# Routed experts of a decoder step: four lanes of 64 rows, or three lanes of 64 and two of 32

## What is computed

```python
def swiglu(x, w_gu, w_down):
    g, u = jnp.split(x @ w_gu, 2, axis=-1)
    return (jax.nn.silu(g) * u) @ w_down
...
yb = lax.map(lambda a: swiglu(a[0], w_e_gu[a[1]], w_e_down[a[1]]), (xb, block_expert))
y = jnp.zeros((N + 1, D), x.dtype).at[slot_token].add(yb.reshape(n_slots, D) * slot_gate[:, None])
```

## Time and profile before

| what | us |
|---|---|
| median of 3 runs | 2894.19 |
| lowest, highest | 2887.44, 2895.16 |
| the profiled execution | 2892.4 |
| its span, first to last instruction | 2890.6 |
| dispatch stage, about | 1858.4 to 1995.4 |
| routed stage, about | 1995.4 to 2791 |
| combine stage | from 2791 on |

### The profile page before, as it was taken

How to read it: one execution, slowest core, us unless ns; L and a number is a source line. 1 busy time by engine, 2 the same in 40 slices (tenths; PEclk the granted TensorE clock), 3 DMA queues, 4 the chain that set the end, 5 groups by cost and what they waited for, 6 DMA issues and landing times. The chain is left out here.

```text
span 2890.6 us, 44067 instructions
## 1 busy us (share of the span) xinstructions
PE 2560.4 (89%) x14550; PEld 1473.9 (51%) x14550; DVE 1507.3 (52%) x3758; ACT 1106.3 (38%) x2384; POOL 372.8 (13%) x419
## 2 busy tenths in 40 slices
PE   4998996979989799986889959797999999999977
PEld 1443443558878687874566634344333333333332
DVE  1456554658878778784888664585111111111126
ACT  1223212659878688783655501121111111111110
POOL 0000000111011000101232121043000000000025
PEclk7999997979999999996999979898999999999988
DMA  8023058622154021207100084215989899897867
GB/s 332 17 77 93 21 159 288 215 82 74 56 200 165 35 76 41 88 1 181 43 26 18 9 270 131 104 44 230 407 330 420 335 352 343 315 386 274 312 248 283
DMA packets 192864, 511.69 MB, mean 177 GB/s; under 512 B 24169, under 2 KB 102315, under 8 KB 160440
## 3 DMA queue, kind: packets, MB, share of 16 engines
q1 hardware_dynamic: 136812, 311.88, 30.2%
q0 software_dynamic: 28640, 127.09, 12.2%
q10 hardware_dynamic: 27252, 70.69, 6.5%
HBM read 631.86 MB, written 86.93 MB: 249 GB/s over the span
## 5 line engine op out<-in xcount | busy, mean ns | idle before, releaser
L2974 PE MATMUL routed_ex_pG<-dispatch_exWG,routed_ex_XT 128*64 128x512 f32 x2048 | 451.1, 597 | 12.8 <-DMA dispatch_exWG<-in_w_e_gu 10.7
L2097 DVE TENSOR_REDUCE ssqc<-SQ 128x8 f32<-128x512 f32 x516 | 346.1, 683 | 116.7 <-ACT SQ L1900 102.5
L1805 PE MATMUL eK<-dWkv,LT 128*128 128x256 f32 x1032 | 316.4, 389 | 12.3 <-ACT SQ L1900 11.8
L1808 PE MATMUL eK<-WA,LT 128*128 128x272 f32 x1032 | 326.9, 399 | 0.0
L1900 ACT ACTIVATE SQ<-eK 128x512 f32<-128x512 f32 x516 | 292.2, 602 | 56.1 <-PE eK L1808 41.2
L2974 PEld LDWEIGHTS routed_ex_pG<-dispatch_exWG,routed_ex_XT 128*64 128x64 f32 x2048 | 147.5, 138 | 310.7 <-issue 310.3
L3065 DVE TENSOR_TENSOR routed_ex_sg<-routed_ex_sg,routed_ex_pG 128x256 f32<-128x256 f32 x64 | 26.9, 421 | 525.9 <-ACT routed_ex_sg L3022 525.9
L556 PE MATMUL in_pp<-ada_Win,in_hT 128*128 128x512 f32 (+1 forms) x640 | 280.7, 597 | 9.8 <-ACT in_pr L454 9.8
L2993 PE MATMUL routed_ex_pY<-routed_ex_WD,routed_ex_AT 128*64 128x512 f32 x1024 | 233.8, 598 | 0.8 <-DMA routed_ex_WD<-in_w_e_down 0.8
L1808 PEld LDWEIGHTS eK<-WA,LT 128*128 128x128 f32 x1032 | 200.7, 194 | 28.9 <-DVE numc L2096 0.2
L1805 PEld LDWEIGHTS eK<-dWkv,LT 128*128 128x128 f32 x1032 | 189.6, 195 | 47.7 <-ACT SQ L1900 17.0
(11 more groups left out here) (551 smaller groups left out, 3738.6 us busy)
## 6 DMA issues: line engine op xcount, KB each, us to landing
dispatch_exWG<-in_w_e_gu SPq DMA_DIRECT2D x256, 1024.0 KB
routed_ex_WD<-in_w_e_down SPq DMA_DIRECT2D x132, 1024.0 KB, 13.0
s_yblk<-routed_ex_Y ACTq DMA_DIRECT2D x64, 512.0 KB
ada_Win<-in_w_ada ACTq DMA_DIRECT2D x8, 2048.0 KB, 12.7
s_yblk<-zrows SPq DMA_DIRECT2D x15, 1024.0 KB
ada_Wada<-in_w_ada SPq DMA_DIRECT2D x8, 1024.0 KB, 15.3
ada_Win<-in_w_in ACTq DMA_DIRECT2D x4, 2048.0 KB, 18.7
dispatch_exWG<-in_w_e_gu SPq DMA_DIRECT2D x4, 2048.0 KB
```

Of the source, the lines that this page charges most:

```text
L1805: pe.matmul(pK[kn % 3][:, 512 + z:512 + z + HK], key, Wkv[:, 4:8, 0:NOPE], start=True, stop=True)
L1808: pe.matmul(pK[kn % 3][:, z:z + HK + 16], key, WA[:, pr, :], start=True, stop=True).then_inc(s_KN, 1)
L2097: dve.tensor_reduce(ssqc[cg % 2][:, n - 1 - tau, :], SQ[kn % 4].rearrange("p (h d) -> p h d", h=H), AX.X, ALU.add).then_inc(s_red, 1)
L2974: m = pe.matmul(pG[u][r, :], XT[u][:, k, r], WG[2 * u + v][:, k, :], start=(k == 0), stop=(k == KD - 1))
```

## The change

Each pair has five lanes: three of 64 rows and two of 32. Block 0 holds lanes 0 and 1 (64 rows each), block 1 holds lane 2 (64 rows) and lanes 3 and 4 (32 rows each, at rows 64 and 96). An expert is cut either into tiles of 64 rows, and goes to the wide lanes, or into tiles of 32, and goes to the narrow ones. Experts with an even number of 32-row tiles stand first in an order, those with an odd number last; the chip computes for every possible dividing point how many pairs the wide and the narrow lanes would need, takes the point where the larger of both is least, and that is `nq`. Positions in the two lists are kept apart by adding `CLASS` to those of the narrow list, and the block and row of each token are computed for both lists and one of them chosen. The largest number of pairs, `NQ`, becomes 46, `NBLK` 92. The first gate/up weights of the fifth lane are loaded at the beginning of the routed stage, ahead of the down weights. Two tensors (`SD`, `lg`) are no longer kept for the whole program, and two of the nine matrices B have a place of their own, which frees and takes SBUF.

The diff, cut to its core:

```diff
@@ -40,8 +40,14 @@
 NEG = -3.0e38
 NC9 = NS + 1
 GRP = 64
-NQ = -(-(NE + (NTOK * TK - NE) // GRP) // 4)
+TILE = 32
+N64, N32 = 3, 2
+NL = N64 + N32
+NQ = -(-(NE + (NTOK * TK - NE) // GRP + -(-NTOK // GRP)) // 4) + 1
 NQ += NQ % 2
+LANE_ROWS = [(v // 2, GRP * (v % 2), GRP) for v in range(N64)] + [(1, GRP * (N64 - 2) + TILE * w, TILE) for w in range(N32)]
+LANES = [[v for v in range(NL) if LANE_ROWS[v][0] == u] for u in range(2)]
+CLASS = 16384
 NBLK = 2 * NQ
 SLOTS = NBLK * P
 BIGM = 1.0e9
...
-        G["expert"] = sb("expert", [5, P], I32)
-        G["loads"] = sb("loads", [1, 4 * NQ], I32)
+        G["expert"] = sb("expert", [NL + 1, P], I32)
+        G["loads"] = sb("loads", [1, NL * NQ], I32)
-        G["SD"] = sb("SD", [P, NS // 2, PAGE + 1])
...
+            if st is stage_prompt:
+                scores_kept = root.enter_context(ExitStack())
+                G["SD"] = scores_kept.enter_context(nc.sbuf_tensor("SD", [P, NS // 2, PAGE + 1], F32, side="right"))
+            if st is stage_out:
+                logits_kept = root.enter_context(ExitStack())
+                G["lg"] = logits_kept.enter_context(nc.sbuf_tensor("lg", [P, NT + 1, NE], F32, side="right"))
...
-            for v in range(4):
+            for v in range(NL):
                 sp.dma_start(G["loads"][0:1, v * NQ:(v + 1) * NQ], G["expert"][v:v + 1, 0:NQ]).then_inc(s_m, 16)
-            sp.dma_start(G["nblk"][0:1, 0:1], G["expert"][4:5, 0:1]).then_inc(s_m, 16)
-            sp.wait_ge(s_m, 80)
+            sp.dma_start(G["nblk"][0:1, 0:1], G["expert"][NL:NL + 1, 0:1]).then_inc(s_m, 16)
+            sp.wait_ge(s_m, 16 * (NL + 1))
             expert = [sp.value_load(G["loads"][0:1, v * NQ:v * NQ + 1], min_val=0, max_val=NE - 1) for v in range(4)]
             sp.wait_ge(s_lt, 1)
             for v in range(4):
...
-            link(dve.tensor_scalar(nbi[:, :], nb[:, :], float(GRP - 1), None, ALU.add))
-            link(dve.tensor_scalar(nbi[:, :], nbi[:, :], 6, None, ALU.arith_shift_right))
-            link(dve.tensor_copy(nb[:, :], nbi[:, :]))
-            link(dve.tensor_tensor_scan(be[:, :], ones[:, :], nb[:, :], 0.0, ALU.mult, ALU.add))
-
-            link(dve.tensor_scalar(nqi[:, :], be[:, NE - 1:NE], 3.0, None, ALU.add))
-            link(dve.tensor_scalar(nqi[:, :], nqi[:, :], 2, None, ALU.arith_shift_right))
-            link(dve.tensor_copy(nq[:, :], nqi[:, :]))
-            for v in range(4):
-                link(dve.tensor_scalar(reach[:, v:v + 1], nq[:, :], float(v), c("part"), ALU.mult, ALU.add))
-                link(dve.tensor_scalar(S1[:, 0, :], be[:, :], reach[:, v:v + 1], 0.0, ALU.is_le, ALU.add, accum_out=eb[:, v:v + 1]))
-                link(dve.tensor_scalar(S1[:, 0, :], be[:, :], reach[:, v:v + 1], 0.0, ALU.is_equal, ALU.add, accum_out=first[:, v:v + 1]))
-            link(dve.tensor_scalar(eb[:, 0:4], eb[:, 0:4], float(NE - 1), None, ALU.min))
+            pair = lambda v: v.unsqueeze(1).to_broadcast([P, 2, NE])
+            for x, (g, bits) in enumerate(((GRP, 6), (TILE, 5))):
+                link(dve.tensor_scalar(nbi[:, :], nb[:, :], float(g - 1), None, ALU.add))
+                link(dve.tensor_scalar(nbi[:, :], nbi[:, :], bits, None, ALU.arith_shift_right))
+                link(dve.tensor_copy(size[:, x, :], nbi[:, :]))
+            link(dve.tensor_scalar(nbi[:, :], nbi[:, :], 1, None, ALU.bitwise_and))
+            link(dve.tensor_copy(odd[:, :], nbi[:, :]))
+            link(dve.tensor_tensor(cum[:, :, :], size[:, :, :], pair(odd[:, :]), ALU.mult))
+            for x in range(2):
+                link(dve.tensor_tensor_scan(odds[:, x, :], ones[:, :], cum[:, x, :], 0.0, ALU.mult, ALU.add))
+            link(dve.tensor_tensor(cum[:, :, :], size[:, :, :], cum[:, :, :], ALU.subtract))
+            for x in range(2):
+                link(dve.tensor_tensor_scan(evens[:, x, :], ones[:, :], cum[:, x, :], 0.0, ALU.mult, ALU.add))
+            last = slice(NE - 1, NE)
+            link(dve.tensor_tensor(total[:, :], evens[:, 1, last], odds[:, 1, last], ALU.add))
+            link(dve.tensor_tensor(cum[:, :, :], odds[:, :, :], evens[:, :, :], ALU.subtract))
+            link(dve.tensor_tensor(cum[:, :, :], cum[:, :, :], evens[:, :, last].to_broadcast([P, 2, NE]), ALU.add))
+            link(dve.tensor_tensor(cum[:, :, :], cum[:, :, :], pair(odd[:, :]), ALU.mult))
+            link(dve.tensor_tensor(cum[:, :, :], cum[:, :, :], evens[:, :, :], ALU.add))
+
+            link(dve.tensor_scalar(nbi[:, :], cum[:, 0, :], float(N64 - 1), {2: 256.0, 3: 171.0}[N64], ALU.add, ALU.mult))
+            link(dve.tensor_scalar(nbi[:, :], nbi[:, :], 9, None, ALU.arith_shift_right))
+            link(dve.tensor_copy(cost[:, :], nbi[:, :]))
+            link(dve.tensor_scalar(rest[:, :], cum[:, 1, :], total[:, 0:1], -1.0, ALU.subtract, ALU.mult))
+            link(dve.tensor_scalar(nbi[:, :], rest[:, :], float(N32 - 1), None, ALU.add))
+            link(dve.tensor_scalar(nbi[:, :], nbi[:, :], N32 // 2, None, ALU.arith_shift_right))
+            link(dve.tensor_copy(rest[:, :], nbi[:, :]))
+            link(dve.tensor_tensor(cost[:, :], cost[:, :], rest[:, :], ALU.max))
+            link(dve.tensor_scalar(cost[:, :], cost[:, :], -1.0, None, ALU.mult))
+            link(dve.tensor_reduce(nq[:, :], cost[:, :], AX.X, ALU.max, negate=True))
+
+            link(dve.tensor_scalar(left[:, :], nq[:, :], float(N64), None, ALU.mult))
+            link(dve.tensor_scalar(wide[:, :], cum[:, 0, :], left[:, 0:1], None, ALU.is_le))
+            link(dve.tensor_tensor(rest[:, :], size[:, 1, :], wide[:, :], ALU.mult))
+            link(dve.tensor_reduce(kept[:, :], rest[:, :], AX.X, ALU.add))
+            link(dve.tensor_scalar(cum[:, 1, :], cum[:, 1, :], kept[:, 0:1], None, ALU.subtract))
...
+            link(dve.tensor_tensor(here, each(start[:, :]), at, ALU.is_equal))
+            link(dve.tensor_tensor(here, here, inside, ALU.mult))
+            link(dve.tensor_reduce(first[:, :], here, AX.X, ALU.add))
+            link(dve.tensor_tensor(here, each(start[:, :]), at, ALU.is_le))
+            link(dve.tensor_tensor(here, here, inside, ALU.mult))
+            link(dve.tensor_tensor(here, here, each(c("iota")[:, 0:NE]), ALU.mult))
+            link(dve.tensor_reduce(eb[:, 0:NL], here, AX.X, ALU.add))
...
+            for x, (g, n) in enumerate(((GRP, N64), (TILE, N32))):
+                for v in range(1, n):
+                    link(dve.tensor_scalar(cut[:, N64 * x + v:N64 * x + v + 1], nq[:, :], float(g * v), None, ALU.mult))
+                link(dve.tensor_scalar(back[:, x:x + 1], nq[:, :], -2.0 * P, float(g), ALU.mult, ALU.add))
...
+            for x, (g, n, to) in enumerate(((GRP, N64, place), (TILE, N32, posf))):
+                k = 2 * P // g
+                link(dve.tensor_scalar(part[:, :, :], slot[:, :, :], g - 1, None, ALU.bitwise_and))
+                link(dve.tensor_copy(lane[:, :, :], part[:, :, :]))
+                link(dve.tensor_scalar(to[:, :, :], low[:, :, :], float(k), float(x * GRP * N64), ALU.mult, ALU.add))
+                link(dve.scalar_tensor_tensor(out=to[:, :, :], in0=lane[:, :, :], scalar=float(1 - k), in1=to[:, :, :], op0=ALU.mult, op1=ALU.add))
+                for v in range(1, n):
+                    link(dve.tensor_scalar(lane[:, :, :], low[:, :, :], cut[:, N64 * x + v:N64 * x + v + 1], back[:, x:x + 1], ALU.is_ge, ALU.mult))
+                    link(dve.tensor_tensor(to[:, :, :], to[:, :, :], lane[:, :, :], ALU.add))
...
+    WG = G["ex_WG"] + [sb(f"{pre}WG{i}", [P, KD, 2 * DE]) for i in range(4, NL)]
+    WD = [sb(f"{pre}WD{i}", [P, 2, D]) for i in range(NL)]
...
+    rows_of = [slice(a, a + w) for _, a, w in LANE_ROWS]
...
-                load = [sp.value_load(G["loads"][0:1, bass.ds(i * 2 + (v * NQ + j), 1)], min_val=0, max_val=2 * NE - 1) for v in range(4)]
+                load = [sp.value_load(G["loads"][0:1, bass.ds(i * 2 + (v * NQ + j), 1)], min_val=0, max_val=2 * NE - 1) for v in range(NL)]
                 for u in range(2):
                     for m, (used, landed) in enumerate(((s_gh, s_w), (s_gu, s_wb))):
                         sp.wait_ge(used, i * 4 + (2 * j + u + 3))
-                        for v in (2 * u, 2 * u + 1):
+                        for v in LANES[u]:
                             if m == 0:
-                                sp.wait_ge(G["s_wg"][v], 16)
+                                sp.wait_ge(s_wg0[v], 16)
...
+                for v in range(NL):
+                    sp.wait_ge(s_y, i * 8 + (4 * j + 2 * LANE_ROWS[v][0] + 5))
...
+            expert = [sp.value_load(G["loads"][0:1, v * NQ:v * NQ + 1], min_val=0, max_val=NE - 1) for v in range(NL)]
+            for v in range(4, NL):
+                sp.dma_start(WG[v][:, :, :], T["w_e_gu"][0, bass.ds(expert[v], 1)].rearrange("a (p k) n -> p (a k) n", p=P)).then_inc(s_wg0[v], 16)
+            for v in range(NL):
...
-                    for v in range(2):
```

(51 more changed lines are left out.)

53 lines of the change are left out of this document (28 added, 25 removed).

## The result

The changed kernel takes 3238.1 us (median of 4 runs, 3237.2 to 3250.4), the kernel before 2890.8 us in the runs made beside it. The ratio is 1.120, its 95% interval 1.118 to 1.122: 12% slower. The profiled execution took 3237.9 us, its span is 3236.0.

What follows compares the result with a forecast made beforehand. PE was taken to bound the routed loop, DMA close behind. 2892.4 - 774.3 (old loop) + 1116 (thirty pairs) + 10 (start) + 3 (end) gave 3247, 3249 against the median; forecast 3248 us, range 2830 to 3300.

Steps and rivals of the forecast that it cites:

- both main cases: Routed loop: either a shape change empties PE (chance 0.70, about 3248 us) or lanes run side by side (0.25, 2844 us).
- Pairs: Routed loop: the new plan needs 30 pairs instead of 32, removing 47.1 us if a pair still takes 23.56.
- A pair: Routed loop: a pair takes 37.2 us instead of 23.56, thirty take 1116.
- step: One k of block 1's matmuls: a wide and a narrow phase, together 1.99 us against 0.86, 12 times a pair.
- The decisive choice: Block 1's matmuls: PE empties itself whenever the shape changes, as at single changes in the earlier trace; chance 0.70.
- Weights: Expert weight loads in the routed loop: SP works 14.2 us a pair, no waits for weights, 0 us added.
- Dispatch: DVE's planning before the routed loop: chain 17 us instead of 6.2, B ending some 20 us later.
- The start of the loop: First routed weights and gate_up after dispatch: +10 us, bounds 0 (all covered) and +20 (none).
- The loop's end: Skipped rounds between the last store's issue and combine, 8 instead of 4: +3 us, bounds 0 and +6.
- (a): Block 1: narrow lanes run beside the wide one, pair stays 23.56 us; 2844 us, range 2830 to 2870; chance 0.25.
- (b): Block 1: the narrow lanes too come one after another, 49 us a pair, total 3605 us; chance 0.03.
- (c): Routed loop: the saving does not come, through another dividing point or late first weights; about 2893 us; chance 0.02.

Runs made afterwards that it cites:

- all32: Changed kernel with the 64 rows of lane 2 issued as two matmuls of 32, so block 1 has one shape: 2861.9 us, ratio 0.988.
- before_block1_split: The control: kernel before, with both lanes of block 1 issued as two matmuls of 32 rows each, one shape: 2907.8 us.
- lanes24: Changed kernel with two lanes of 64 in block 0, four of 32 in block 1, part of z moved through DRAM: 2832.7 us, ratio 0.979.
- down_mixed: Changed kernel with lane 2 issued in 32s in gate_up alone; down still mixes 64 and 32: 2974.8 us.
- grouped: Changed kernel, block 1 reordered: in each half of gate_up and down all wide-lane steps first, then all narrow ones: 3171.6 us.
- before_lane3_split: Kernel before, with only the second lane of block 1 issued as two matmuls of 32 beside one of 64: 3304.5 us.
- all32_nopool: Changed kernel with block 1 all in 32s, without POOL's products for the shared expert's output; leaves work out: 2841.0 us.

## Why the prediction was right

Forecast 3248, measured 3238; faster was given 0.26 and slower 0.73. The stated range, 2830 to 3300, held both main cases, so its being met says little; what tells is the pair, its step and the rows of the profile.

**Pairs.** 30 forecast, 30 measured. **A pair.** 37.2 forecast, 36.94 measured; step 1.99 forecast, 1.99 in the rows above. The decisive choice, that the gap of the earlier trace rows holds for all changes and not only for those between overlapping columns, was right, and the control and the split of lane 3 show it without the rest of the change. The forecast was a little high because 23.56 + 12 x 1.13 = 37.12 was rounded up to 37.2, and because it charged a change on both sides of all 12 steps: block 1's first wide step in `gate_up` follows block 0's own 128*64, so a pair has 23 changes more than before and not 24. The rows of single changes in the trace before were enough to price a loop of them: 0.49 + 0.52 for the wide phase, 0.46 + 0.52 for the narrow one.

The rule of the Trainium skill (TensorEngine Tiling (Array Packing), Key Properties), that a change of tiling mode drains TensorE, holds here: in `gate_up` of block 1 the first load of the other shape stands behind 0.81 or 0.84 us without a load, where it is 0.29 or 0.30 us within one shape. The pairs of eight kernels fit one sum: 23.56 + 0.86 for each step whose wide and narrow part come one after another + 0.134 for each change of shape beyond the four that a pair of the kernel before has.

| kernel | steps in two phases | changes a pair | sum | measured |
|---|---|---|---|---|
| before | 0 | 4 | 23.56 | 23.56 |
| `all32`, `before_block1_split`, `lanes24` | 0 | 6 | 23.83 | 23.84 |
| `down_mixed` | 4 | 13 | 28.21 | 28.21 |
| `grouped` | 12 | 11 | 34.82 | 34.79 |
| changed, `before_lane3_split` | 12 | 27 | 36.96 | 36.94, 36.93 |

The 0.86 is from the earlier trace rows, the 0.134 from `grouped` against the changed kernel, 2.15 us for 16 changes. The other rows then follow within 0.03. Of the 13.4 us that a pair became longer, 10.3 are lost overlap and 3.1 are changes.

**Weights.** 0 forecast, none seen. Counted as the forecast counted, by the waits for PE, SP works (1109.8 - 349.0 - 335.8)/30 = 14.2 us a pair, forecast 14.2; without its waits for DMA too it is 13.7:

```profile
SPq L2987 <- PE routed_ex_pG L3059: 349.0, 58, 7.0
SPq L2992 <- PE routed_ex_pY L3078: 335.8, 58, 8.4
SPq L2991 <- DMA routed_ex_WD<-in_w_e_down: 15.2, 5, 4.0
```

**Dispatch.** Here the sum was right by luck. DVE's chain: 17 us forecast, 27.9 measured. The step that failed priced each instruction from rows in which POOL ran none of its products of 1024 columns. Without them the chain takes 19.3 (`all32_nopool`), so some 2 us were short in the prices themselves, and 8.6 are POOL's. Behind the chain, up to B's end, 9 more were forecast (places of tokens 4, wider B 0.7, POOL's products 4), and it became 0.9 shorter. POOL's busy time in these two windows tells why, first before, then after (busy time of POOL, clock, DMA share, GB/s):

```profile
1901.00:1907.18 6.18, 1.45 (x2) 1.00 0.19 76
1907.18:1961.57 54.39, 31.83 (x19) 1.00 0.09 30
```

```profile
1899.70:1927.63 27.93, 13.78 (x10) 1.00 0.16 54
1927.63:1981.15 53.52, 26.25 (x14) 0.89 0.03 11
```

A longer chain takes in 12.3 us more of POOL's products, and 5.6 less of them fall behind it. What POOL leaves free behind the chain is 27.3 us instead of 22.6, and the 4.7 more are what the forecast had for the places and the wider B; this fits with DVE being held up by POOL in both stretches, but only the chain was tried without POOL's products. B's end was forecast 20 us later and is 19.6 later (1961.57, 1981.15), PE ends `lists()` 9.5 us later (forecast 7). The start of the loop: +10 forecast, +11.0 by the rows, +12.3 from the chain's start.

**The loop's end.** +3 forecast, +3.2 measured. **The rest.** The sum was 9.2 us too high: 6.2 in the loop (the pair 0.26 too long, thirty times, less 1.6 of first and last pair), 4.2 in combine, whose code is the same in both, and 1.3 ahead of the chain, less 2.3 at the start and 0.2 at the loop's end. The 4.2 have no known cause; the three kernels with the old dispatch differ there by up to 3.9 among themselves.

**The rivals.** (a) *Side by side* is refuted by the loads of the profile after: the narrow ones wait 0.81 us for a wide phase on other columns. As the price of a loop without the mix its range was right and its 2844 was 18 us low: `all32` with the same plan took 2861.9, within the rival's 2830 to 2870. (b) fell with the narrow loads that stand in fours, (c) with the 60 sigmoids.

## What to carry to other kernels

Matmuls side by side in the array should be of one tile shape: 128*64 and 128*32 never overlapped here, though on different columns (other mixes were not tried). A saving of 6% of the rounds was turned into a loss of 12% by a block that alternates two. Where lanes of different width share a block, issue the wide one as several of the narrow shape: the extra matmuls cost nothing here, four abreast took the 0.43 us of two. Before pricing a chain of short DVE instructions, look at what POOL runs in that stretch.
